# Token halves, one pass over the attention weights and modulation rows on TensorE, in a two-block layer kernel

## What is computed

```python
mod = c @ w_ada[layer] + b_ada[layer]
shift, scale, gate = [t[:, None, :] for t in jnp.split(mod, 3, axis=-1)]
h = _rmsnorm(x, norm_g[layer]) * (1.0 + scale) + shift
...
u = jax.nn.silu(_layernorm(u, conv_ln_g[layer], conv_ln_b[layer]))
y_conv = (u * jax.nn.silu(z_conv)) @ w_conv_out[layer]
...
wts = [d_g * jnp.exp(m_g - m_all) for m_g, d_g in zip(maxes, dens)]
w_sum = wts[0] + wts[1] + wts[2]
att = (wts[0][..., None] * outs[0] + wts[1][..., None] * outs[1]
       + wts[2][..., None] * outs[2]) / w_sum[..., None]
y_att = (att * jax.nn.silu(z_att)) @ w_att_out[layer]
merged = jax.nn.sigmoid(g_conv) * y_conv + jax.nn.sigmoid(g_att) * y_att
x = x + gate * (merged @ w_o[layer])
...
merged = (g_pool * jnp.einsum('bsc,cd->bsd', y_pool, w_branch_pool[l])
          + g_attn * jnp.einsum('bsc,cd->bsd', y_attn, w_branch_attn[l]))
```

## Time and profile before

| | us |
|---|---|
| runs | 2748.93, 2745.04, 2749.23 (median 2748.93) |
| profiled execution | 2745.55, its span 2743.8 |
| PE busy | 2616.0 (95%) |
| DVE busy | 1386.1 (51%) |
| POOL busy | 896.5 (33%) |
| ACT busy | 599.9 (22%) |
| mean granted clock | 0.981 |

### The profile page before, as it was taken

How to read it: one execution, slowest core, us unless ns; L and a number is a source line. 1 busy time by engine, 2 the same in 40 slices (tenths; PEclk the granted TensorE clock), 3 DMA queues, 4 the chain that set the end, 5 groups by cost and what they waited for, 6 DMA issues and landing times.

```text
span 2743.8 us, 32992 instructions
## 1 busy us (share of the span) xinstructions
PE 2616.0 (95%) x12424; PEld 2196.8 (80%) x12424; DVE 1386.1 (51%) x2422; ACT 599.9 (22%) x1361; POOL 896.5 (33%) x870
## 2 busy tenths in 40 slices
PE   6999999999999998969999899989999999999997
PEld 5787889978899877747788778878778888888886
DVE  5611348977777774771563611134373343434336
ACT  3212221123211323430132033230141011010102
POOL 3422213422434241314344222223233333333333
PEclk9999999999999999989999999999999999999999
DMA  6311221222312233633342032234241111111113
GB/s 229 106 46 46 72 73 36 67 70 78 117 39 63 82 107 121 194 125 129 103 150 86 16 97 70 73 112 142 64 155 51 54 46 46 46 46 52 52 57 123
DMA packets 153635, 236.03 MB, mean 86 GB/s; under 512 B 22818, under 2 KB 67618, under 8 KB 153508
## 3 DMA queue, kind: packets, MB, share of 16 engines
q1 hardware_dynamic: 152356, 230.14, 26.8%
q10 hardware_dynamic: 1152, 4.19, 0.4%
HBM read 181.65 MB, written 52.63 MB: 85 GB/s over the span
## 4 chain that ended last, share of the span: by engine, by line
PE 85%; DVE 9%; DMA 3%; ACT 1%; issue 1%; POOL 1%; SPq 0%; POOLq 0%; DVEq 0%; ACTq 0%
PE ps L1825 51%; PE ps L2019 12%; PE ps L2051 12%; PE ps L1937 3%; PE ps L1913 2%; DVE scr L1383 2%; PE ps L1923 2%; PE ps L1854 2%; DMA small<-st_d 1%; DMA scr<-in_x 1%; DVE act_lo L1256 1%; DVE scr L1498 0%; DVE scr L1276 0%; POOL w_lo L895 0%; DVE big L1746 0%
## 5 line engine op out<-in xcount | busy, mean ns | idle before, releaser
L893 POOL CAST w_hi<-raw 128x512 fp32r<-128x512 f32 x416 | 306.9, 738 | 1780.0 <-DMA raw<-in_w_in 841.9
L895 POOL TENSOR_TENSOR w_lo<-raw,w_hi 128x512 fp32r<-128x512 f32 x416 | 578.8, 1391 | 33.3
L1825 PE MATMUL ps<-act_hi,w_hi 128*128 128x512 f32 x1344 | 543.5, 404 | 36.5 <-DVE act_lo L1256 34.3
L1825 PE MATMUL ps<-act_lo,w_hi 128*128 128x512 f32 x1344 | 537.7, 400 | 0.0
L1825 PE MATMUL ps<-act_hi,w_lo 128*128 128x512 f32 x1344 | 529.7, 394 | 0.0
L1383 DVE SCALAR_TENSOR_TENSOR scr<-scr,small 128x512 f32<-128x512 f32 x480 | 431.0, 898 | 15.6
L1825 PE MATMUL ps<-w_hi,act_hi 128*128 128x512 f32 (+1 forms) x960 | 388.9, 405 | 13.4 <-DVE act_lo L1256 10.9
L1825 PE MATMUL ps<-w_lo,act_hi 128*128 128x512 f32 (+1 forms) x960 | 377.4, 393 | 0.0
L1825 PE MATMUL ps<-w_hi,act_lo 128*128 128x512 f32 (+1 forms) x960 | 377.2, 393 | 0.0
L1825 PEld LDWEIGHTS ps<-act_hi,w_hi 128*128 128x128 f32 x1344 | 256.1, 191 | 99.0 <-issue 44.8
L1825 PEld LDWEIGHTS ps<-act_lo,w_hi 128*128 128x128 f32 x1344 | 255.2, 190 | 57.6 <-issue 4.6
(11 more groups left out here) (185 smaller groups left out, 2749.9 us busy)
## 6 DMA issues: line engine op xcount, KB each, us to landing
raw<-in_w_in SPq DMA_DIRECT2D x176, 256.0 KB, 3.3
raw<-in_w_up SPq DMA_DIRECT2D x64, 256.0 KB, 2.7
raw<-in_w_down SPq DMA_DIRECT2D x64, 256.0 KB, 2.6
vreg<-in_w_ada SPq DMA_DIRECT2D x48, 256.0 KB, 4.1
raw<-in_w_in SPq DMA_DIRECT2D x72, 128.0 KB, 2.3
x_d<-big SPq DMA_DIRECT2D x16, 512.0 KB, 3.0
scr<-x_d SPq DMA_DIRECT2D x16, 512.0 KB, 4.2
o_d<-scr SPq DMA_DIRECT2D x48, 128.0 KB, 2.2
```

The source lines that it names most:

```text
L893: pool.tensor_copy(dhi, src).then_inc(w_hi_done, 1)
L895: pool.tensor_tensor(dlo, src, dhi.bitcast(F32), ALU.subtract).then_inc(w_ready, 1)
L1825: ins = nc.tensor.matmul(out_, lhs, rhs, start=(m == 0), stop=(m == 3 * nk - 1))
```

## The change

The order of the units changes and with it the work behind it.

- Start: pieces n = 1 and n = 3 both go through PE as rows: one column of `c` stationary, `ada` moving, 512 fp32 columns into one row of a free PSUM bank, 16 matmuls. Eight come before the lead, four behind each of the first two k steps. ACT copies the two rows out, eight small matmuls make columns of them (`row_cols`) behind the third k step. `mod_cols(0)` goes between the transposes of x. The first weight pieces are fetched later (behind `ada` piece 14 instead of 9).
- Stage Z begins with a `zc` unit. The second token half of all eight `zc` tiles comes first and is stored; the first half comes from block 3 on, isn't stored, and is gated in place: `norm_tanh` on ACT into the one buffer `tt0`, `norm_gate` on DVE, 512 columns each.
- The attention statistics of all blocks are loaded at once, and one pass makes the weights of all blocks (in the space of `cosT`, `sinT`). `za` is loaded whole (2 MB) into `attzT`.
- `yc`, `ya`, `yp`, `yb` run over all tiles of the first token half, then of the second. Splits are made by half, and the gates of the second half of the layer norm run beside `yc` of the first.

```diff
-ADA_SUM = {key: i + 1 for i, key in enumerate([key for key in ADA if key[0] != 1])}
+ADA_SUM = {key: i + 1 for i, key in enumerate([key for key in ADA if key[0] not in (1, 3)])}
+ADA_ROW = {key: i + 1 for i, key in enumerate([key for key in ADA if key[0] in (1, 3)])}
...
+    gates = [("zc", t, 1) for t in range(8)] + [("zc", t, 0) for t in range(8)]
+    items.extend(("store" if u[2] else "gate", u) for u in gates)
+    units.append(gates[0])
+    for B in range(NB):
+        units += [("ct", B, 0), ("ct", B, 1), gates[2 * B + 1], ("lt", B, 0), ("lt", B, 1)]
+        units += gates[2 * B + 2:2 * B + 3] + [("at", B, 0)]
+    units += half_units("yc")
...
+            def prefetch_z(n):
+
+                for _ in range(2 if n % 16 < 4 else 1 if n % 16 < 8 or n % 16 >= 12 else 0):
+                    next_piece()
...
-                sp.dma_start(sg, st_d[:, rows, :].rearrange("g p c -> p g c")).then_inc(o_ld, 16)
-                sp.dma_start(zab.rearrange("p (k s) -> p k s", k=4),
-                             gate_d["za"].rearrange("(k p) s -> p k s", p=P)[:, :, P * B:P * B + P]
-                             ).then_inc(za_ld, 16)
-
+
+            prefetch_z(0)
...
             conv_block(0)
+            for g in range(NG):
+                sp.dma_start(sg[:, g], st_d[g].rearrange("(b p) c -> p b c", p=P)).then_inc(sg_ld, 16)
             attention_block(0)
+            sp.dma_start(attzT, gate_d["za"].rearrange("(k p) s -> p k s", p=P)).then_inc(za_ld, 16)
...
+            def z_load(t):
+                if t >= 2:
+                    sp.wait_ge(uz_w, 8 + t - 1)
+                sp.dma_start(zt[t % 2], feature_tile(gate_d["zc"], t, 1)).then_inc(z_ld[t % 2], 16)
...
+            us = unit_range(("yc", 0, 0), ("ya", 7, 1))
+            for i in range(4):
+                gate_load(i, None, us[i], "gc")
+            for i, u in enumerate(us):
+                if i < 16:
+                    prefetch_z(i)
+                else:
+                    prefetch(u)
+                if i < 6:
+                    z_load(i + 2)
+                if i >= 4:
+                    gate_load(i, None, u, "gc" if u[0] == "yc" else "ga")
...
                 split_hi(("h", k), act_hi[:, k, :], featT[:, k, :])
+                if k == 3:
+                    for n in (1, 3):
+                        act.wait_ge(ada_mm, ADA_ROW[(n, 7)])
+                        nc.scalar.activation(mod_row[n], ps_row[n], ACT.Copy).then_inc(row_out, 1)
...
+            def norm_tanh(k, dst, cols):
+                nc.scalar.activation(dst, featT[:, k, cols], ACT.Tanh, scale=c_lgh[:, k:k + 1],
+                                     bias=c_lbh[:, k:k + 1]).then_inc(uz_t, 1)
...
                 elif name == "zc":
+                    if h == 0:
+                        if B == 0:
+                            wait_evac(act, ("lt", 3, 1))
+                        else:
+                            act.wait_ge(uz_w, B)
+                        norm_tanh(B, tt0, first)
                     f_unit(u)
...
+            def norm_gate(n, k, cols, t, z):
+                x = featT[:, k, cols]
+                dve.wait_ge(uz_t, n + 1)
+                link(nc.vector.tensor_scalar(x, x, c_lg[:, k:k + 1], c_lb[:, k:k + 1], ALU.mult, ALU.add))
+                link(nc.vector.scalar_tensor_tensor(x, t, 1.0, x, ALU.add, ALU.mult))
+                if n >= 8:
+                    dve.wait_ge(z_ld[k % 2], 16 * (k // 2 + 1))
+                nc.vector.scalar_tensor_tensor(x, x, 0.25, z, ALU.mult, ALU.mult).then_inc(uz_w, 1)
...
+            for k in range(KT):
+                half_lo("uz", k, 0, featT)
+            for k in range(KT):
+                norm_gate(8 + k, k, second, tt[k % 2], zt[k % 2])
+                if k >= 1:
+                    half_lo("uz", k - 1, 1, featT)
+                if k == 5:
+                    for t in range(4):
+                        conv_gated(t, 0)
+                if k == 6:
+                    conv_gated(4, 0)
...
+            REST = {("yc", 0, 1): ("uz", 7, 1), ("ya", 0, 1): ("az", 3, 1), ("wo", 4, 0): ("mg", 7, 1),
+                    ("w2", 4, 0): ("m2", 7, 1)}
...
+            def mod_piece(n, k):
+                p = ADA.index((n, k))
                 pe.wait_ge(ada_ld[p % RING], 16 * (p // RING + 1))
...
+                nc.tensor.matmul(ps_row[n], small[:, k:k + 1], ada[:, p % RING, :], start=(k == 0),
+                                 stop=(k == KT - 1)).then_inc(ada_mm, 1)
+
+            def row_cols():
+                pe.wait_ge(row_out, 2)
+                for n in (1, 3):
+                    for i in range(4):
+                        ins = nc.tensor.matmul(ps_s[1][:, 4 * n + i:4 * n + i + 1], mod_row[n][:, P * i:P * i + P],
+                                               ones[0:1, :], start=False, stop=True, skip_group_check=True)
+                ins.then_inc(ada_col, 1)
...
+            rows = [key for key in ADA if key in ADA_ROW]
+            for key in rows[0:8]:
+                mod_piece(*key)
             for k in range(KT):
                 for u in lead:
                     for m in range(3 * k, 3 * k + 3):
                         proj(u, m)
...
+                if k < 2:
+                    for key in rows[8 + 4 * k:12 + 4 * k]:
+                        mod_piece(*key)
+                elif k == 2:
+                    row_cols()
```

## The result

The changed kernel takes 2718.85 us (median of four executions, 2716.88 to 2724.86) against 2747.75 us for the kernel before beside it: a ratio of 0.9899, 95% interval 0.9883 to 0.9914. That is 28.9 us less, where 39 were forecast. The profiled execution took 2716.88 us with a span of 2715.1 us, 28.7 less than before.

The account below looks back on a forecast made before the run. PE was taken as the bound, busy 95% of the span, with 128 us of waits plus slow-clock losses; savings of 5 + 6.5 + 3.0 + 3.2 + 7.9 + 13.8 = 39.4 us from 2748.93 gave 2710 us, range 2697 to 2726.

Parts of the forecast that it names:

- case A: Whole kernel: the forecast itself, 2702 to 2718 us, with waits listed singly and halves ready before wanted; chance 0.55.
- case B: Start and stage Z: rows hold the lead back, gate loop near 17 us, 2723 us; chance 0.20.
- Start: Modulation rows and lead: `mod_half(1)` 4.1 us earlier plus 1 us from later weight prefetch, together 5 us saved.
- Entry, attention weights, gates in stage Z: Stage Z: 6.5 us from running `zc` first, 3.0 from one-pass attention weights, 3.2 from gates on chip.
- as the text said it might: PE's clock: new waits may bring back slow stretches; add 3 us if bank waits of 1.2 to 2.4 us do too.
- The loop: Stage Z, blocks 4 to 6: one `at` evacuation to the next takes 15.05 us, 16.3 beside POOL.
- I use the measured mean instead: Stage Z: DVE operations beside POOL priced at the products' mean, 1074 ns, instead of waiting for a whole split.
- `yc`: Branches by halves: the five waits behind the 15.37 us go, saving 7.9 us; slow clock at the start stays.
- least room: `yc(0,0)` bank: wanted 21.8 us after the start, when DVE is at its sixth gate, 19 to 21 us.
- `ya`, `wo`, `w2`: Last stages: first units find their half split already, so waits and slow clock go, 13.8 us (8.8 without the clock).
- Rival D: Gate loop: nine DVE operations per block each wait for a whole POOL split, loop 27.6 us, 2760 us; chance 0.04.
- Rival C: Stage Z and start: gate loop stays at PE's 13.5 us and the start gets more, 2699 us; chance 0.18.

Follow-up runs that it names:

- start_only: Kernel before with only the change's new start (modulation rows 1 and 3 as row matmuls, later weight fetch, `mod_cols(0)` between transposes): 2741.10 us, ratio 0.998.
- the eleven traces: One profiled execution each of the changed kernel, its repeat, its edited variants and the kernel before with the new start alone; all have the new start.
- evac_k4: Changed kernel with DVE's four evacuations of the first output tiles' first half one gate earlier, behind the fifth gate: 2717.84 us, ratio 0.9896.
- short_splits: Changed kernel with POOL's splits of the `yc` weights cut to one column: 2702.70 us, ratio to before 0.9834.
- at_first: Changed kernel with DVE evacuating `at` ahead of the second gate unit's norm and gate in blocks 3 to 6: 2710.64 us, ratio 0.9865.
- after_again: The changed kernel itself, unedited, run once more later (the second trace): 2724.17 us, ratio 0.9919.

## Why the prediction came out as it did

It forecast faster, 2710 us, within 2697 to 2726. The direction and the range held; the likeliest case, 2702 to 2718, was missed by 0.9 us at 2718.85 and by 6 at 2724.17. The result lies between case A and case B (2723). Point by point, by the profiled executions, where 39.4 us were summed and 28.7 came:

- **Start: forecast 5, measured 6.4** at the end of `za` in the first trace, 2.5 in the second, and 5.5 by the time of start_only. Over the eleven traces it is 1.3 to 7.3, mean 4.2, so the 5 was right in size and the 6.4 was luck by some 2 us. The price of a row matmul was nearly right: eight of them took 8.69 us on the partly slow clock and four took 3.59. `mod_half(1)` began at 62.05 us, 7.0 us earlier and not 4.1, because PE reached the rows at 35.6 instead of 37.0 and took 26.5 us to the end of `row_cols` instead of 28.0. PE did wait for the rope tables, 2.60 us, and the 8 us from 80 on ran at a granted clock of 0.79, 1.7 us that were in no term. PE's timeline of the changed kernel, in place of the earlier trace rows:

```profile
35.57 8.69 PE L1959 MATMUL ps<-vreg,small 128*1 128x512 f32 x16
47.14 3.59 PE L1959 MATMUL ps<-vreg,small 128*1 128x512 f32 x8
...
80.07 1.11 PE L1946 MATMUL ps<-ident,scr 128*128 128x128 f32 x4 [2.60 <-DVE scr L1426]
```

- **Entry, attention weights, gates in stage Z: forecast 6.5 + 3.0 + 3.2 = 12.7, measured 2.9** (139.33 to 136.46; 4.3 by the second trace). This is where the forecast failed, by 9.8 us. The entry's wait was 3.3 us and not 2.3 to 2.6: behind two weight loads the `c_d` load took 4.9 us from issue to landing, against 3.8 in the kernel before, 1.1 us more where 0.8 were put; the rest of the difference is not traced. The stage's other waits are 18.3 us and not 14.4. And the clock fell behind the longer ones, as the text said it might, with 3 us for it outside the sum. Stretches of the changed kernel, PE only (us, busy, granted clock, DMA share, GB/s):

```profile
1062.00:1070.00 8.00, 6.19 (x19) 0.57 0.98 261
1158.00:1166.00 8.00, 7.95 (x32) 0.79 0.38 131
...
1220.00:1227.00 7.00, 6.60 (x23) 0.76 0.70 195
```

  After 3.27 us without work the entry's 8 us ran at 0.57. That is 3.4 us by the row, but PE still waited in the first 1.8 us of it; counted from the matmuls' starts 2.9 us were lost, where 1.6 were left in the sum. After the wait of 4.64 us it was 0.79 and 1.7 us. These are 2.9 - 1.6 + 1.7 = 3.0 us of clock, 0.8 of the entry's wait and 3.9 of the others: 7.7 of the 9.8; the rest is not traced. The loop that I summed at 15.05 us measured 15.2 where POOL was idle: right. Beside POOL I put 16.3 (the terms give 16.45). With two single pieces beside it the loop was 16.6 (1159.94 to 1176.55), as put; beside the burst of five it was 20.7. The step that failed: "I use the measured mean instead" for the products, and nothing for the gates. A mean over a stage in which POOL is busy 31% of the time, in pieces that stand apart, says little of a burst of five pieces, and the change moved the weights' splits into bursts (1143 to 1155 us, where the pieces before came in ones and twos).

- **`yc`: forecast 7.9, measured 3.4** (100.1 to 96.7). The waits of low halves went, all of them. But the step "least room", the bank of `yc(0,0)` wanted 21.8 us after the start with DVE at its sixth gate after 19 to 21, had its gates at 2.6 us each. At up to 5.17 us they took 25.1 us, and with 4 us of low halves ahead of them the evacuations began 29.0 us after the start. PE itself came 2.8 us later than put, on the slow clock of the stage's start, and still waited 5.2 us, with some 1.5 us of clock behind it in the last stretch above. The same paragraph timed POOL's splits to that very interval, 20 us from the start, and did not put the two together; that is the lesson of the case. evac_k4 and short_splits both show it: 5 us and 8 to 9 us off `yc`.

- **`ya`, `wo`, `w2`: forecast 13.8, measured 13.9** (5.0 + 4.4 + 4.5 by the table; the 2.1 us more between `yc` and the end lie in no place that the change touches, and start_only shows 1.4 of them as well). No wait stands in these places any more, and no slow clock. The sum of waits and clock held to 0.1 us: each term is a wait that was read off the list, with the clock of its own stretch.

Rival D, the lock that makes it slower, had the right mechanism and too high a price: one DVE operation in the reach of a POOL instruction pays 0.3 to 1.1 us, not 1.39, and POOL has bursts of 5 and 8 pieces in the stretch and not one beside every operation. Rival B came near in size for the wrong reasons: the loop near 17 us was to come from the length of chains, and the start was to give nothing. Rival C (the loop at PE's 13.5 us) was reached by at_first where POOL is idle, 13.9 us.

What remains open: attention weights in one pass and the halves in the second block were not tried alone; what they gave is read from the waits that went. Of the spread in the first 200 us the wait that makes most of it is seen, its cause is not.

## What to carry to other kernels

When a change moves vector work, lay its new place over GpSimd's timeline and price each operation that falls beside a burst at its length there (here 5.17 us for 2.6), not at the stage's mean. Behind every wait that you list, put the slow clock that follows it into the sum. And when a loop has a load in it, issue what the load waits for first: here that order alone was worth 8 us, a quarter again of what the whole change brought.

## What was not expected of the hardware

- DVE with operands in SBUF and POOL slow each other instruction by instruction: 0.69 to 1.66 or 0.98 us on DVE, 0.61 to 1.07 us for a cast on POOL. The operation of DVE with one SBUF input and a per-partition column is hit too, 0.54 to 0.83 and 1.47 us. With one input from PSUM it isn't: 0.67 to 0.69 us in all 11 that overlap POOL. Which operation pays depends on how the two streams meet: in after_again the one-column operation takes 1.47 to 1.52 us in every tile of the burst and the low half 1.09, where the first trace has mostly 0.83 and 1.78.
- A one-row fp32 matmul of 512 columns costs PE 0.90 us (3.59 us for four), four times what one of the 512-column matmuls in the last stage takes, though it yields one row.
- Waits of PE of 2.60, 3.27, 4.64 and 5.18 us were each followed by a stretch at a granted clock of 0.57 to 0.79, a mix of the levels of 1.2 and 2.4 GHz. The trace agrees with the Trainium skill (page "TensorE: Matmul & The Clock Gate", section "Part 1: The HAM clock gate") that idle time brings the lower level. With the clock, the wait of 5.2 us cost some 30% more than its row in the list of waits says, and the one of 3.3 us nearly twice as much.
